# A decoder layer on one core: the compressed branch's probabilities stacked by heads, one value pass per head instead of two

## The reference, cut to what matters

```python
D_MODEL, SEQ = 1024, 512
NSA_HEADS, NSA_KV_GROUPS, NSA_HEAD_DIM = 16, 4, 64
CMP_BLOCK, CMP_STRIDE = 32, 16
...
s_c = jnp.einsum('bgrqd,bgcd->bgrqc', qb, kc).astype(f32)
d_c = t[:, None] - cmp_end[None, :]
vis_c = d_c >= 0
p_c = masked_softmax(s_c - slopes * d_c, vis_c) * jnp.any(vis_c, axis=-1, keepdims=True)
o_c = jnp.einsum('bgrqc,bgcd->bgrqd', p_c.astype(vc.dtype), vc)
...
return gb[..., 0:1] * o_c + gb[..., 1:2] * o_s + gb[..., 2:3] * o_w
```

## Time and profile before

| what | value |
|---|---|
| median of 3 runs | 1270.92 us (1270.31 to 1271.76) |
| the profiled execution | 1270.06 us |
| its span, first to last instruction | 1268.3 us |
| TensorE (PE) busy | 1249.5 us, 99% |
| weight loads (PEld) busy | 1056.3 us, 83% |
| VectorE (DVE) busy | 835.0 us, 66% |
| ScalarE (ACT) busy | 630.5 us, 50% |
| GpSimd (POOL) busy | 88.3 us, 7% |
| chain that ended last | PE 82%, DVE 14%, ACT 2% |

### The profile page before, as it was taken

The page is one execution under the profiler, slowest core; times in us unless marked ns, Lnnn a source line. Parts: engine busy times, 40 slices in busy tenths (PEclk is TensorE's granted clock), DMA queues, the critical chain, the costliest instruction groups (busy, mean ns, idle before and its releaser), DMA issues.

```text
span 1268.3 us, 17700 instructions
## 1 busy us (share of the span) xinstructions
PE 1249.5 (99%) x6709; PEld 1056.3 (83%) x6709; DVE 835.0 (66%) x1585; ACT 630.5 (50%) x1193; POOL 88.3 (7%) x78
## 2 busy tenths in 40 slices
PE   6999999999999999999999999999999999999998
PEld 5998898889978998878877888878888888888887
DVE  4426996899869995998673533333787887874221
ACT  6515667667776768666765532223432322323110
POOL 1000001400051002400030000000000000000000
PEclk9999999999999999999999999999999999999999
DMA  8612322141213221132117533335133233233231
GB/s 238 164 35 57 84 59 56 37 117 53 56 43 100 66 61 42 51 100 76 43 43 252 170 101 95 88 101 164 54 98 100 84 99 98 85 101 133 100 126 41
DMA packets 185593, 116.34 MB, mean 92 GB/s; under 512 B 25917, under 2 KB 169637, under 8 KB 185509
## 3 DMA queue, kind: packets, MB, share of 16 engines
q1 hardware_dynamic: 181879, 108.86, 29.5%
q10 hardware_dynamic: 3630, 6.35, 1.3%
HBM read 106.80 MB, written 8.39 MB: 91 GB/s over the span
## 4 chain that ended last, share of the span: by engine, by line
PE 82%; DVE 14%; ACT 2%; issue 1%; DMA 1%; SPq 0%; DVEq 0%; ACTq 0%
PE g L599 15%; PE g L600 15%; PE g L601 15%; PE t L592 4%; PE g L640 3%; PE g L642 3%; PE g L641 3%; DVE w_low L1538 2%; DVE piece_a L1764 2%; PE ob L789 2%; PE s L953 2%; PE s L954 2%; PE s L955 2%; PE s L773 2%; DVE piece_b L1823 1%
## 5 line engine op out<-in xcount | busy, mean ns | idle before, releaser
L1022 ACT ACTIVATE w_high<-wraw 128x1024 fp32r<-128x1024 f32 x175 | 185.1, 1059 | 290.1 <-DMA wraw<-in_ffn_w_up 142.6
L1538 DVE TENSOR_TENSOR w_low<-wraw,w_high 128x1024 fp32r<-128x1024 f32 x174 | 216.7, 1248 | 128.9 <-ACT w_high L1022 126.6
L599 PE MATMUL g<-hT_hi,w_high 128*128 128x512 f32 x360 | 159.4, 443 | 0.3 <-issue 0.3
L640 PE MATMUL g<-w_high,hT_hi 128*128 128x256 f32 x512 | 151.7, 296 | 0.1
L642 PE MATMUL g<-w_high,hT_lo 128*128 128x256 f32 x512 | 144.3, 282 | 0.0
L641 PE MATMUL g<-w_low,hT_hi 128*128 128x256 f32 x512 | 144.2, 282 | 0.0
L601 PE MATMUL g<-hT_hi,w_low 128*128 128x512 f32 x360 | 142.6, 396 | 0.0
L600 PE MATMUL g<-hT_lo,w_high 128*128 128x512 f32 x360 | 142.6, 396 | 0.0
L599 PE MATMUL g<-h2T_hi,w_high 128*128 128x512 f32 x352 | 140.0, 398 | 0.0
L600 PE MATMUL g<-h2T_lo,w_high 128*128 128x512 f32 x352 | 139.7, 397 | 0.0
L601 PE MATMUL g<-h2T_hi,w_low 128*128 128x512 f32 x352 | 139.7, 397 | 0.0
(11 more groups left out here) (347 smaller groups left out, 2525.9 us busy)
## 6 DMA issues: line engine op xcount, KB each, us to landing
wraw<-in_w_in SPq DMA_DIRECT2D x152, 256.0 KB, 3.2
wraw<-in_ffn_w_up SPq DMA_DIRECT2D x88, 256.0 KB, 3.2
wraw<-in_ffn_w_down SPq DMA_DIRECT2D x44, 256.0 KB, 3.0
wraw<-in_w_proj_b SPq DMA_DIRECT2D x32, 256.0 KB, 3.1
yT_lo<-spill SPq DMA_DIRECT2D x6, 1024.0 KB, 9.4
spill<-piece_e ACTq DMA_DIRECT2D x16, 256.0 KB, 4.2
wraw<-in_w_proj_a SPq DMA_DIRECT2D x16, 256.0 KB, 3.2
wraw<-in_w_out SPq DMA_DIRECT2D x16, 256.0 KB, 3.3
```

The source lines that it names most:

```text
L599: nc.tensor.matmul(gb[par][:, :], w, hi, start=k == 0, stop=False)
L640: nc.tensor.matmul(out_, hT[0][:, k, cols], w, start=k == 0, stop=False)
L1022: nc.scalar.activation(whi[slot_of(u)][:, :, :], wraw[u % 2][:, :, :], ACT.Copy).then_inc(w_hi, 1)
L1538: V.tensor_tensor(wlo[slot_of(u)][:, :, :], wraw[u % 2][:, :, :], whi[slot_of(u)][:, :, :].bitcast(F32), ALU.subtract).then_inc(w_lo, 1)
```

## The change

The two tiles of `pcT` are no longer the rounded and the low part of all heads, but the heads 0 and 1 in the first and 2 and 3 in the second. Of `pcT[0]` rows 0 to 63 hold the rounded part of heads 0 and 1, where the transposition leaves them, and rows 64 to 127 their low part, which VectorE writes across from the lower to the upper rows. `pcT[1]` is the mirror image: heads 2 and 3 are rounded in rows 64 to 127, and low in rows 0 to 63. So head r's low part lies at row 32 ((r + 2) mod 4), and `vcg[:, r]` gets the rounded values there too, in columns 0 to 63; columns 64 to 127 of these rows stay zero. One pass over 512 columns per head now gives rounded probabilities times rounded and low values, and low probabilities times rounded values. The product of the two low parts is left out.

```diff
-        pcT = [sb(f"pcT_{n}", [P, T], F32R, ph1) for n in ("hi", "lo")]
+        pcT = [sb(f"pcT_{n}", [P, T], F32R, ph1) for n in ("heads01", "heads23")]
...
-                        for part in pcT:
-                            ins = nc.tensor.matmul(ob[:, :], vcg[:, r, :, :].rearrange("p a d -> p (a d)"), part[:, :],
-                                                   start=False, stop=part is pcT[1])
+                        ins = nc.tensor.matmul(ob[:, :], vcg[:, r, :, :].rearrange("p a d -> p (a d)"),
+                                               pcT[r // 2][:, :], start=False, stop=True)
...
-                            nc.scalar.activation(pcT[0][:, 256 * q:256 * (q + 1)], tb[par][:, 0:256], ACT.Copy).then_inc(pcT_hi, 1)
+                            for half in range(2):
+                                rows = slice(DH * half, DH * (half + 1))
+                                nc.scalar.activation(pcT[half][rows, 256 * q:256 * (q + 1)], tb[par][rows, 0:256],
+                                                     ACT.Copy).then_inc(pcT_hi, 1)
...
-                    ins_ = V.tensor_copy(vcg[32 * r:32 * r + NC, r, :, :], vc_all[:, g, :, :].bitcast(F32))
+                    seq.done(V.tensor_copy(vcg[32 * r:32 * r + NC, r, :, :], vc_all[:, g, :, :].bitcast(F32)))
+                    low = 32 * ((r + 2) % R)
+                    ins_ = V.tensor_copy(vcg[low:low + NC, r, 0, :], vc_all[:, g, 0, :].bitcast(F32))
...
-                        dve.wait_ge(pcT_hi, g * 2 + (q + 1))
+                        dve.wait_ge(pcT_hi, g * 4 + (2 * q + 2))
                         cols = slice(256 * q, 256 * (q + 1))
-                        V.tensor_tensor(pcT[1][:, cols], tb[T_(K_CMP + q) % 2][:, 0:256], pcT[0][:, cols].bitcast(F32),
-                                        ALU.subtract).then_inc(t_rel, 1)
+                        for half in range(2):
+                            rows, other = (slice(DH * h, DH * (h + 1)) for h in (half, 1 - half))
+                            V.tensor_tensor(pcT[half][other, cols], tb[T_(K_CMP + q) % 2][rows, 0:256],
+                                            pcT[half][rows, cols].bitcast(F32), ALU.subtract).then_inc(pcT_lo, 1)
+                        dve.wait_ge(pcT_lo, g * 4 + (2 * q + 2))
+                        dve.sem_inc(t_rel, 1)
```

More of the change, by code:

```diff
@@ L283, in program @@
             "am_ready", "seg_fill", "seg_exp", "m_ready", "ymm"))
-        am_lo, adt_split, qk_rooted = sem("am_lo"), sem("adt_split"), sem("qk_rooted")
+        am_lo, adt_split, qk_rooted, pcT_lo = sem("am_lo"), sem("adt_split"), sem("qk_rooted"), sem("pcT_lo")
         xdt_made, sq_summed = sem("xdt_made"), sem("sq_summed")
```

## The result

The changed kernel takes 1278.93 us (median of five runs; four lie between 1278.54 and 1279.24, while one took 2470.4 us, as no other run of these kernels did; it is left out of the ratio below, and without it the median is 1278.88). Before it is 1270.74 in the same comparison. The ratio is 1.0064, 95% interval 1.0051 to 1.0077: slower by 0.6%, 8.2 us. The forecast was 1278.8, made from a median before of 1270.92.

A forecast was written before the change was run, and what follows sets the result against it. VectorE paces units n = 0 to 3, TensorE the rest of the scan. Delays of 0.84 + 1.77 = 2.61 us a group, 10.44 over four, minus 2.56 gained: 7.88 slower than 1270.92, so 1278.8 us; range 1274.0 to 1281.0.

The forecast's parts named there:

- What bounds the kernel: VectorE sets the pace in units n = 0 to 3, TensorE from n = 4 to the end of the scan.
- The casts: End of unit n = 0: four 31x64 value copies added between the four 31x128, 0.84 us a group, all going through.
- The low parts: Unit n = 1: VectorE starts 0.40 us later, four subtractions take 2.04 us, 1.37 more; 1.77 us a group in all.
- the lower bound: Copies pipeline (0.40 for four), low parts keep pitch 0.335 (+1.14), ScalarE keeps 0.28: 1.82 us a group, 1275.6 us.
- the second place: The low parts in unit n = 1, where VectorE's added work delays TensorE's transposes in n = 2 by 1.77 us.
- The gains: 16 passes removed at 0.23 us: head 0's gives nothing; 0.69 a group in groups 0 to 2, 0.49 in group 3; 2.56.
- The signs to look for: Transposes wait 0.8 us longer at n = 1, 1.2 twice at n = 2; TensorE busy 4 us less; VectorE's later waits unchanged.
- VectorE's spare 0.24: Unit n = 4: VectorE waited 0.78 us where 0.54 is usual after a TensorE wait, so head 1's 0.23 counts.
- A: Rival: TensorE is the bound everywhere, each of 16 passes gives 0.23 us, 3.7 faster, 1267.2 us; chance 0.08.
- B: Rival: instructions on other partition halves overlap as others do, half the loss, 1275.6 us; chance 0.15.
- C: Rival: no change to speak of, later slack takes up some three quarters of the delays; chance 0.04.
- D: Rival: worse than 1281 us from a new wait, for instance ScalarE's 1.05 us reaching the weights' high halves; chance 0.03.

The follow-up runs named there:

- pass_off: The kernel before, without the second compressed pass of every head (over the low part), VectorE and ScalarE work unchanged: 1267.94 us, ratio 0.9979.
- before_pool: The kernel before, with its four value casts of a group on GpSimd at the start of the group: 1267.68 us, ratio 0.9975.
- pass_kept: The changed kernel with a second pass per head over the same operands, all its VectorE and ScalarE work kept: 1281.80 us, ratio 1.0085.
- four_casts: The changed kernel without the four added 31x64 casts per group: 1275.72 us, ratio 1.0042 against the kernel before.
- half_order: The changed kernel with VectorE's half subtractions in the other order, upper half first: 1278.29 us, ratio 1.0060 against the kernel before.
- all_three: The changed kernel with value casts on GpSimd, a wait per half, one release, and upper half first on VectorE and ScalarE: 1269.50 us, ratio 0.9991.

## Why the prediction was right, point by point

**What bounds the kernel.** Shown: in pass_off head 0's pass goes into a longer wait in every group, before_pool gives 3.1 us without touching TensorE, and pass_kept prices the moved work at 11.2 us, where the sum had 10.44.

**The number.** That the forecast came within 0.2 us is in part luck. The cost was put 0.7 us too low (11.2 against 10.44), the gain 0.3 too low (2.9 against 2.56), and the median from which it was reckoned was 0.2 above that of the comparison (1270.92 against 1270.74). These errors nearly cancel.

**The casts.** 0.87 us a group for 0.84. A 31x64 cast takes 0.186 rather than 0.18, with the same gap. four_casts makes it 3.2 us for the four groups, where the sum had 3.36.

**The low parts.** 0.40 later, as put; 2.05 us for 2.04. The price of the alternating halves was taken from q's low heads, and that choice between the bounds is what made the number: the lower bound's pitch of 0.335 (+1.14 us a group) would have missed 0.24 us a group, and its start 0.12 more.

**What was missed.** In n = 2 the delay is 298.94 - 293.99 = 4.95 us, and 280.73 - 277.68 = 3.05 stood at n = 1, so the second place costs 1.90 where 1.77 was put. The difference is the 0.12 us of the held score reduction, a consequence of reading PSUM's upper half last that I had not looked for; half_order shows it. It makes 0.5 us over the four groups. With this term the forecast would have been 1279.3: a better sum, and a number further off.

**The gains.** From group 1's n = 3 to the first cast of group 2 (415.65 before, 420.12 now) the delay falls from 4.95 to 4.47 us, by 0.48, not 0.69. This is the one group in which TensorE waits 0.42 us for ScalarE's copy of the convolved tile (the wait list's last line), which I had not foreseen. Every kernel here with the stacked parts has this one wait of 0.4 us, and none with the rounded and low tiles; its cause stays open. In group 0 it falls from 2.84 (VectorE's tile 2 of n = 2 starts at 158.81, before at 155.97) to 2.18 at group 1's first cast, 0.66 for the 0.69 put. In group 2 it falls from 7.25 (440.19 - 432.94) to 6.31 at group 3's first cast (561.08 - 554.77), by 0.94, and from group 3's 9.09 (581.05 - 571.96) to the 8.8 of the span, by 0.3 for the 0.49 put. That makes 2.4 us in this pair of traces. Over the four groups the passes were worth 2.7 and 2.9 us by two runs, against 2.56. So the size of the gain is right, but not its division among the groups; why group 2 gives more than its three passes of 0.23 stays open.

**The signs to look for.** The waits at the transposes came where they were put: 0.83 at n = 1, 1.03 and 1.14 at n = 2, and nothing new at n = 3. Two were off. TensorE's busy time fell by 3.0 us and not by 4; in pass_off, which has the same 16 passes less and no new place at which TensorE waits, it fell by 3.5. The likely reason, not tested: the record of the matmul ahead of a wait is 0.28 us long where the next one would start after 0.12, so each of the seven new waits adds up to 0.16 us of time that counts as busy. And VectorE's waits from n = 4 on did change, group 1's n = 4 and n = 6:

```profile
319.57 0.62 DVE L1839 TENSOR_TENSOR pT_lo<-t,pT_hi 128x256 fp32r<-128x256 f32 x2 [0.55 <-ACT pT_hi L1325]
...
338.80 0.62 DVE L1839 TENSOR_TENSOR pT_lo<-t,pT_hi 128x256 fp32r<-128x256 f32 x2 [0.80 <-ACT pT_hi L1325]
```

The first was 0.78 before. The second was 1.16:

```profile
334.33 0.62 DVE L1835 TENSOR_TENSOR pT_lo<-t,pT_hi 128x256 fp32r<-128x256 f32 x2 [1.16 <-ACT pT_hi L1326]
```

Head 1's pass made TensorE earlier by 0.23, and that used up VectorE's spare 0.24, by the sum's own working; I should have said so among the signs. At 0.55 us that wait is down to what it is where TensorE itself has waited, so more passes taken off ahead of that transpose would not be expected to gain anything there; no run tests it.

**The rivals.** A (every pass counts, faster) falls with head 0's pass in pass_off, with before_pool and with the sign of the result. B (narrow instructions overlap) falls with the timeline: four half copies in 1.59 us at 0.38 each, four half subtractions in 1.89 with a wait between the pairs and 1.78 without it at 0.42 each. C and D did not occur: ScalarE's 1.05 us more shows up in no wait of TensorE in n = 1 to 3.

## What to carry to other kernels

Before trading TensorE's work against VectorE's, look at who waits for whom at the very place where each half of the trade lands: here the vector work landed ahead of a transpose that was already waiting and cost its whole price, while the first of the passes taken off landed ahead of the same transpose and was worth nothing. Splitting a copy or a subtraction by partitions saves no time on either engine, and doubles their number: a 64x256 instruction lasts as long as a 128x256 one (0.42 us on VectorE, 0.38 on ScalarE), and alternating halves also lose the overlap. If a few small copies stand in a stretch that VectorE paces, an engine that idles may take them: 0.99 us of casts a group on GpSimd gave 3.1 us over the four groups.

## What the runs showed of the hardware that I had not expected

A vector instruction that reads PSUM at another start partition than the last PSUM reader started only after the instruction in front of it had finished, even though that last reader lay nine vector instructions back and all between them read SBUF alone: 1.31 us from scaling to reduction against 1.19 with the halves in the other order. The Trainium skill has this rule, in "VectorE: DVE Perf Modes", section "Two Vector instructions with no wait between them": for PSUM and for SBUF apart, it remembers in which group of 32 partitions the last instruction that read from that memory started. The trace agrees, and had I applied it to what follows the new instructions, not only to them, the missing 0.5 us would have been in the sum.

ScalarE shows something alike: copies that alternate between partition halves start every 0.40 us, where full-height ones of the same 256 columns start after 0.28. It is the alternation and not the height: in all_three, where the lower half is copied last, the full-height instruction behind the copies overlaps the last of them by 0.10 us, while in the changed kernel, where the upper half is last, it starts 0.02 us behind it. In all_three:

```profile
283.91 1.59 ACT L1351 ACTIVATE pcT_heads<-t 64x256 fp32r<-64x256 f32 x4 [0.88 <-PE t L604]
285.40 0.50 ACT L1300 ACTIVATE piece_b<-piece_a,negmx 128x256 f32<-128x256 f32 x1
```
